# Router loads from ScalarE's queue, and two expert tiles ahead of the first rows, in a two-layer hybrid decoder

## The chip, the cores and the metric

The kernel runs on one core of a Trainium2 chip. The metric is device time in microseconds (us). All times inside a run come from one profiled execution, counted from the start of its span. The five engines are TensorE (PE, with its weight loads as PEld), VectorE (DVE), ScalarE (ACT), GpSimd (POOL) and SyncE (SP), which here issues DMA. Three queues carry most DMA: q1 is what SP issues, q10 what ScalarE issues, q0 what GpSimd issues; 16 DMA engines serve them all.

## What is computed

Two residual layers on 1024 tokens of width 1024, all in float32. The first mixes by attention, the second by a state-space layer and gated DeltaNet; both are followed by a mixture of experts and a gated embedding. What matters here:

```python
for i in range(DEPTH):                      # DEPTH = 2
    a = _rms_norm(h, norm_mix[i])
    ...
    h = h + mixer(a) @ w_out                # even_mixer or odd_mixer
    h = h + _hier_moe(_rms_norm(h, norm_ffn[i]), ...)
    h = h + _per_layer_embedding(h, p[i], ...)

def _hier_moe(m, ...):
    g_prob = softmax(m @ w_group + b_group)           # 4 groups, the best one is taken
    e_logits = (m @ w_expert + b_expert)[group]       # 8 experts in it, the best two are taken
    ...
    return _expert_dispatch(xf, experts, weights, w_gate, w_up, w_down)
    # each expert: (silu(x @ w_gate[e]) * (x @ w_up[e])) @ w_down[e]
```

There are 32 experts; the three weight matrices of one are 2 MB each.

## The kernel before

Tokens lie in 8 tiles of 128 rows (`NT`), a row's 1024 columns in two halves of 512 (`SLAB`). Engines meet only at semaphores; a block ends with a barrier of all engines. The order within an engine is the order of the code.

`mixer_end` is one block, run once a layer. For each tile i TensorE multiplies the mixer's output by `w_out`, half by half (`product(i, 0, ...)` with slab 0, `product(i, 1, ...)` with slab 1, eight steps k each), VectorE adds the residual (`add`), which SP loads into `h` in four pairs of tiles. TensorE transposes the sum (`turn`), ScalarE and VectorE copy the two halves (`copy`), and TensorE multiplies by the router weights `w` (`score`). VectorE multiplies `w` once by the gain column first (`scale_router`, in the turn of tile 0, waits for all five small loads, `router_in`). ScalarE squares the sum for the norm (`square`, `root`); VectorE scales a tile by norm and gains into `m` (`scale`), picks two experts for each token (`choose`) and numbers their slots (`place`), with ranks from TensorE (`rank_tokens`). GpSimd scatters the rows of the tile to `slots_in` in HBM. For the last tile ScalarE multiplies by the norm and GpSimd by the gains (L1542).

In the second layer (`delta`) half of the product's input must first be normed (`scale_o` on VectorE, with `root_o` on ScalarE), transposed on TensorE (`turn_o`) and copied on ScalarE (`copy_o`).

After the last tile come small steps on 32 experts: they are sorted by count, and `r.table` is written, whose row 3 holds which expert has which rank (L1511). SP waits for the scatters and reads the first two experts' rows (L1231). `keep_busy` issues products of the identity into a bank that nobody reads.

What SP issues in `mixer_end`, in this order: slab 1, `h`, gains and the five router loads (L1217 to L1222), then own loads (L1226): the first six weight tiles of the experts, four of them at once in the first layer and three in the second, the rest when the last products are done.

`first_blocks` computes the experts in 21 units. Weight tiles pass through a ring of eight places in the order of `weight_order`. The six tiles of experts 0 and 1 (`FIXED`) are the own loads; from number 6 on SP reads the expert's index from `r.table` and issues each tile when TensorE has finished with what lies in its place:

```python
before = [x for x in range(n) if places[x] == places[n]]
if before:
    used, by = tiles[before[-1]][0], last_user[tiles[before[-1]]]
    sp.wait_ge((gated, upped, downed)[used], (2 if used == 2 else 1) * (by + 1))
```

TensorE's first instruction there is the transpose of unit 0's rows (`turn(0)`, L1760), which waits for the read of L1231. In the trace a gate or up tile shows as `in_moe_w_gate_dram` or `in_moe_w_up_dram`, a down tile as `in_moe_w_down_dram`; tiles of the ring lie in `place`, `xt`, `s_t`, `own`, `gdn_t`, `work` and `gbz`.

Of the kernel before, what the change touches and what calls it, by code (L numbers as in the profile page):

```python
# [15 lines left out]
P = 128  # L16
# [139 lines left out]
def row(ap1d):  # L156

    return ap1d.rearrange("(a n) -> a n", a=1)
# [843 lines left out]
def even_mixer(nc, c, t, h, layer, r, xt, s5_t, after):  # L1002
# [5 lines left out]
    with ExitStack() as ctx:  # L1008
# [14 lines left out]
        def pair_out(heads):  # L1023
# [19 lines left out]
        mixer_end(nc, c, t, layer, h, t["x"][0], lambda k, i: mixed_t[k][:, i], slabs, [(slabs[1], slab_of(t["ev_w_out"][j], SLAB))], m, normed, mt, spare,  # L1043
                  preloads(t, layer, ring), 4, r, ch, gains=gains)
# [7 lines left out]
def constants(nc, ctx):  # L1052
# [10 lines left out]
    c.scattered_before = [0] * 4  # L1063
    c.rows_in = [ctx.enter_context(nc.semaphore(f"rows_in{n}")) for n in range(4)]
# [13 lines left out]
EARLY = 6  # L1078
# [77 lines left out]
def mixer_end(nc, c, t, layer, h, residual, columns, slabs, slab_loads, first_rows, m, mt, spare, own_loads, early_loads, r, ch, delta=None, gains=None):  # L1156
# [10 lines left out]
    with ExitStack() as ctx:  # L1167
        if gains is None:
# [29 lines left out]
        names = ("residual0_in", "residual1_in", "residual2_in", "residual3_in", "slabs_in", "router_in", "gain_in", "own_in", "iota_done",  # L1198
                 "o_means", "o_roots", "o_scaled", "o_turned", "o_copied", "products", "added", "squares", "means",
                 "roots", "rstd_made", "normed", "scaled", "router_scaled", "turns", "copied_act", "copied_dve", "scored", "taken_two", "ranked", "placed", "counted", "shifted",  # L1200
                 "exped", "sorted_at", "tabled", "positions", "positions_turned", "earlier_made", "spread_out", "vec_steps")
        with stage(nc, *names) as (block, sems):
# [6 lines left out]
            def _(sp):  # L1209
                with nc.allow_non_contiguous_dma(reason="router weights, short rows, column slabs"):  # L1210
                    for tile, view in slab_loads:
                        sp.dma_start(tile, view).then_inc(z["slabs_in"], 16)
                    sp.dma_start(h[:, 0:2], residual.rearrange("(t p) d -> p t d", p=P)[:, 0:2]).then_inc(residual_in[0], 16)
                    for n in range(1, 4):
                        two = slice(2 * n, 2 * n + 2)
                        sp.dma_start(h[:, two], residual.rearrange("(t p) d -> p t d", p=P)[:, two]).then_inc(residual_in[n], 16)
                    sp.dma_start(gains, row(t["norm_ffn"][layer]).to_broadcast([P, D])).then_inc(z["gain_in"], 16)  # L1217
                    sp.dma_start(gain_col[:], t["norm_ffn"][layer].rearrange("(k p) -> p k", p=P)).then_inc(z["router_in"], 16)
                    sp.dma_start(w[:, :, 0:GROUPS], t["moe_w_group"][layer].rearrange("(k p) n -> p k n", p=P)).then_inc(z["router_in"], 16)
                    sp.dma_start(w[:, :, GROUPS:ROUTES], t["moe_w_expert"][layer].rearrange("(k p) n -> p k n", p=P)).then_inc(z["router_in"], 16)  # L1220
                    sp.dma_start(bias[:, 0:GROUPS], row(t["moe_b_group"][layer]).to_broadcast([P, GROUPS])).then_inc(z["router_in"], 16)
                    sp.dma_start(bias[:, GROUPS:ROUTES], row(t["moe_b_expert"][layer]).to_broadcast([P, EXPERTS])).then_inc(z["router_in"], 16)  # L1222
# [12 lines left out]
            def _(pe):  # L1235
# [8 lines left out]
                def product(i, n, ks):  # L1244
                    if i and ks[0] == 0:
                        pe.wait_ge(z["added"], 2 * (i - 1) + n + 1)
                    if i == 0 and n == 1 and ks[0] == 0 and slab_loads:
                        pe.wait_ge(z["slabs_in"], 16 * len(slab_loads))
# [54 lines left out]
                keep_busy(pe, c, o_bank, 24)  # L1303
# [13 lines left out]
                keep_busy(pe, c, o_bank, 10)  # L1317

            @block.scalar
            def _(act):  # L1320
# [16 lines left out]
                def square(i, n):  # L1337
                    half = slice(n * SLAB, (n + 1) * SLAB)
                    act.wait_ge(z["added"], 2 * i + n + 1)
                    if n == 0 and i >= RING_M:  # L1340
                        act.wait_ge(scattered[i % RING_M], before[i % RING_M] + 32 * (i // RING_M))
                    act.activation(m[:, i % RING_M, half], h[:, i, half], ACT.Square, scale=1.0 / math.sqrt(D), accum_out=half_ms[:, i, n:n + 1]).then_inc(z["squares"], 1)
# [5 lines left out]
                if delta is not None:  # L1348
                    root_o(0)
                    copy_o(0)  # L1350
                for i in range(NT):
# [7 lines left out]
                    root(i)  # L1359
                act.wait_ge(z["rstd_made"], NT)  # L1360
                act.activation(m[:, (NT - 1) % RING_M, :], h[:, NT - 1, :], ACT.Copy, scale=rstd[:, NT - 1:NT]).then_inc(z["normed"], 1)
# [5 lines left out]
            def _(dve):  # L1367
# [26 lines left out]

                def scale(i):
                    if i == 0:
                        dve.wait_ge(z["gain_in"], 16)
# [65 lines left out]
                for i in range(NT):  # L1463
# [3 lines left out]
                    if i:  # L1467
                        choose(i - 1)
                        place(i - 1)
# [2070 lines left out]
```

## Time and profile before

| What | us |
|---|---|
| median of 3 runs | 2957.79 |
| lowest, highest | 2955.67, 2961.13 |
| the profiled execution | 2960.23 |
| its span | 2958.6 |
| TensorE busy | 2760.8 (93%) |
| TensorE weight loads busy | 1417.6 (48%) |
| VectorE busy | 1090.9 (37%) |
| ScalarE busy | 674.3 (23%) |
| GpSimd busy | 229.4 (8%) |

`mixer_end` starts at about 660 us in the first layer and 2100 us in the second; `first_blocks` starts at about 819 and 2263. The page shows each engine's busy time in 40 slices of the span, and what DMA moved: 404 to 418 GB/s in the slices that lie wholly in the experts' stages. A busy share is an average over stages; what a change is worth is read at the waits of its own stage. In a row of the timeline the bracket tells how long the engine was idle before it and what released it.

### The profile page before, as it was taken

Reading aid. Unit: us, or ns where it says so; the run is one execution under the profiler, and the core shown is the slowest. Engines: PE = TensorE matmul, PEld = TensorE weight load, DVE = VectorE, ACT = ScalarE, POOL = GpSimd, SP = SyncE. Lnnn points to the kernel's source line nnn. Section 1 sums busy time; section 2 is a strip of 40 time slices with the busy share of each in tenths; the row PEclk is TensorE's granted clock in tenths of the full one; section 3 lists DMA queues with packets and bytes.
Section 4 is the critical chain, followed back from the end, with each engine's and each line's share of the span. In section 5 each row is a group of like instructions: output and inputs, shape, how many; then the busy total and the mean of one; then the engine's idle time right before and its main releaser. Section 6 shows DMA issues by size and latency. Waiting matters only on the chain. (4 is left out here: it accounts for less than half of the span.)

```text
span 2958.6 us, 41299 instructions
## 1 busy us (share of the span) xinstructions
PE 2760.8 (93%) x16673; PEld 1417.6 (48%) x16674; DVE 1090.9 (37%) x2394; ACT 674.3 (23%) x1312; POOL 229.4 (8%) x288
## 2 busy tenths in 40 slices
PE   8999999999999999999989899988999989999998
PEld 5544555555543233334457744488655323232344
DVE  3585455553510000004456635555563000000053
ACT  3310354541110000002420123333211000000132
POOL 0000000000100000002000000055211000000020
PEclk9999999999999999999999999999999999999999
DMA  4000693006399999997110120000517999999931
GB/s 167 29 29 0 244 408 116 1 19 233 127 344 409 412 409 411 409 414 278 43 47 29 17 72 29 0 3 25 200 57 266 387 408 409 406 413 404 392 129 43
DMA packets 139127, 609.40 MB, mean 206 GB/s; under 512 B 27780, under 2 KB 34340, under 8 KB 122536
## 3 DMA queue, kind: packets, MB, share of 16 engines
q1 hardware_dynamic: 115976, 529.59, 45.7%
q0 software_dynamic: 15296, 53.49, 4.9%
q10 hardware_dynamic: 7664, 23.66, 2.1%
q8 instruction: 134, 2.20, 0.3%
q14 instruction: 57, 0.47, 0.0%
HBM read 503.81 MB, written 101.71 MB: 205 GB/s over the span
## 5 line engine op out<-in xcount | busy, mean ns | idle before, releaser
L2857 PE MATMUL acc<-xt,work 128*128 128x512 f32 x384 | 166.9, 593 | 0.0
L695 PE MATMUL acc<-h,xt 128*128 128x512 f32 x384 | 165.2, 592 | 0.0
L328 PE MATMUL scores<-xt 65*128 65x512 f32 (+7 forms) x384 | 146.0, 489 | 0.4 <-DVE xt L469 0.4
L1768 PE MATMUL pu<-place 128*32 128x512 f32 (+2 forms) x912 | 141.4, 628 | 0.6 <-issue 0.6
L1768 PE MATMUL py<-place 128*32 128x512 f32 (+2 forms) x672 | 126.5, 615 | 12.5 <-issue 12.4
L1768 PE MATMUL pg<-place 128*32 128x512 f32 (+1 forms) x528 | 130.4, 594 | 0.0
L475 DVE TENSOR_REDUCE nmax<-scores 128x1 f32<-128x256 f32 (+7 forms) x128 | 96.8, 757 | 73.9 <-PE scores L330 71.8
L1252 PE MATMUL acc<-place 128*128 128x512 f32 x256 | 118.0, 605 | 2.5 <-DMA place<-in_ev_w_out_dram 1.4
L695 PEld LDWEIGHTS acc<-h,xt 128*128 128x128 f32 x384 | 72.9, 190 | 91.1 <-issue 90.9
L2857 PEld LDWEIGHTS acc<-xt,work 128*128 128x128 f32 x384 | 72.0, 190 | 86.1 <-issue 86.1
L1863 DVE COPY work<-py 128x512 f32<-128x512 f32 x21 | 14.5, 692 | 226.6 <-PE py L1768 226.6
L1863 DVE COPY place<-py 128x512 f32<-128x512 f32 x21 | 14.5, 692 | 225.4 <-PE py L1768 225.4
L422 ACT ACTIVATE s_t<-scores,nmax 128x256 f32<-128x256 f32 (+7 forms) x128 | 94.3, 737 | 8.0 <-DVE nmax L475 6.6
L792 ACT ACTIVATE place<-acc 128x256 f32<-128x256 f32 (+4 forms) x88 | 39.9, 473 | 239.6 <-PE acc L695 239.5
L2505 PE MATMUL acc<-s_t,xt 128*128 128x260 f32 (+1 forms) x256 | 85.4, 495 | 1.1 <-PEq L71 1.1
L1896 DVE TENSOR_TENSOR work<-work,pu 128x512 f32<-128x512 f32 x21 | 14.4, 687 | 192.5 <-PE pu L1768 192.5
L1896 DVE TENSOR_TENSOR place<-place,pu 128x512 f32<-128x512 f32 x21 | 14.4, 688 | 189.4 <-PE pu L1768 189.4
L1768 PEld LDWEIGHTS py<-place 128*32 128x32 f32 (+2 forms) x672 | 39.8, 120 | 89.1 <-issue 87.8
L1842 ACT ACTIVATE work<-pg 128x512 f32<-128x512 f32 x21 | 12.5, 597 | 290.7 <-PE pg L1768 290.7
L328 PEld LDWEIGHTS scores<-xt 65*128 65x128 f32 (+1 forms) x384 | 62.8, 190 | 33.1 <-issue 32.7
L1842 ACT ACTIVATE place<-pg 128x512 f32<-128x512 f32 x21 | 12.5, 597 | 289.2 <-PE pg L1768 289.2
L1768 PE MATMUL pg<-own,work 128*32 128x512 f32 (+2 forms) x400 | 74.0, 599 | 3.6 <-issue 2.5
(755 smaller groups left out, 5467.1 us busy)
## 6 DMA issues: line engine op xcount, KB each, us to landing
place<-in_moe_w_up_dram SPq DMA_DIRECT2D x25, 2048.0 KB, 25.7
slots_out<-zeros SPq DMA_DIRECT2D x4, 9216.0 KB, 63.0
place<-in_moe_w_down_dram SPq DMA_DIRECT2D x18, 2048.0 KB, 25.8
xt<-in_moe_w_up_dram SPq DMA_DIRECT2D x17, 2048.0 KB, 25.3
xt<-in_moe_w_gate_dram SPq DMA_DIRECT2D x16, 2048.0 KB, 23.9
place<-in_moe_w_gate_dram SPq DMA_DIRECT2D x16, 2048.0 KB, 23.4
xt<-in_moe_w_down_dram SPq DMA_DIRECT2D x15, 2048.0 KB, 27.6
s_t<-in_moe_w_gate_dram SPq DMA_DIRECT2D x10, 2048.0 KB, 24.3
```

The source lines that it names most:

```text
L328: pe.matmul(bank(n, u)[:, a * SLAB:a * SLAB + w], qkt[0:kind(p).rows, p % 2, u, 0, i * P:(i + 1) * P], qkt[0:kind(p).rows, p % 2, u, 1, a ...
L422: act.activation(probs[:, u, n % 2, 0:(i + 1) * P], bank(n, u), ACT.Exp, bias=nmax[:, n % 2, u:u + 1], accum_out=total[:, (n // NT) % 2, i ...
L475: dve.tensor_reduce(nmax[:, n % 2, u:u + 1], bank(n, u), AX.X, ALU.max, negate=True).then_inc(maxed, 1)
L695: last = pe.matmul(acc[:, n % 4, 0:width], xs[:, k, tile_of(i)], weights[:, k, cols], start=(k == 0), stop=(k == k_of - 1))
L792: last = act.activation(place, part, ACT.Copy)
L1252: last = pe.matmul(acc[:, n, :], columns(k, i), slabs[n][:, k, :], start=(k == 0), stop=(k == KD - 1), skip_group_check=True)
L1768: last = pe.matmul(out[part], lhs[:, k, part], weights_of(kind, q)[:, k, cols], start=(k == 0), stop=(k == k_last), skip_group_check=True)
L1842: act.activation(gate, pg[:], ACT.Silu).then_inc(silued, 1)
L1863: dve.tensor_copy(y[:, n % 2, SLAB:D], py[:, SLAB:D]).then_inc(y_dve, 1)
L1896: dve.tensor_tensor(hid, gate, pu[:], ALU.mult).then_inc(hidden, 1)
L2505: ins = pe.matmul(acc[:, n % 4, 0:width], xt[:, k, at], slab[:, k, 0:width], start=(k == 0), stop=(k == KD - 1))
L2857: last = pe.matmul(acc[:, n % 4, :], slabs[m // 4 % 2][:, k, (m % 4) * P:(m % 4 + 1) * P], xt[:, k, half * SLAB:(half + 1) * SLAB], start= ...
```

## The change

Both layers, in `mixer_end` and at its seam with `first_blocks`:

- SP no longer issues gains and router loads; ScalarE does, ahead of its loop over the tiles (in the second layer behind `root_o(0)` and `copy_o(0)`). SP's own loads follow directly on `h`.
- Slab 1 comes in two DMAs of four steps k each, with a semaphore each.
- In the second layer `turn_o(0)` stands behind the first four products.
- `square` writes its unused output to a PSUM bank, `junk`, and no longer to `m`; the wait for the scatter moves to `scale`.
- For the last tile VectorE multiplies the sum by the gains in two halves (`gain_last`) before the norm is known, ScalarE then by the norm, and GpSimd's product goes.
- The table's row 3 is written first, with a semaphore `listed`. SP waits for it, reads two indices and issues ring tiles 6 and 7 (`LISTED`), then waits for the scatters and reads the first rows. `first_blocks` starts at tile 8.
- Three `keep_busy` runs: 24 becomes 16, 10 becomes 5; those of 5 and 8 stay.

```diff
             @block.sync
...
-                    for tile, view in slab_loads:
-                        sp.dma_start(tile, view).then_inc(z["slabs_in"], 16)
...
-                    sp.dma_start(gains, row(t["norm_ffn"][layer]).to_broadcast([P, D])).then_inc(z["gain_in"], 16)
-                    sp.dma_start(gain_col[:], t["norm_ffn"][layer].rearrange("(k p) -> p k", p=P)).then_inc(z["router_in"], 16)
...
+                    sp.dma_start(slabs[1][:, 0:4], last_slab[:, 0:4]).then_inc(z["slab_head_in"], 16)
+                    sp.dma_start(slabs[1][:, 4:8], last_slab[:, 4:8]).then_inc(z["slab_tail_in"], 16)
...
                 clear_used(sp)
+                views = expert_weights(t, layer)
+                sp.wait_ge(z["listed"], 1)
+                for n, (tile, kind, q) in enumerate(listed_loads):
+                    expert = sp.value_load(r.table[0:1, 3, q:q + 1], min_val=0, max_val=EXPERTS - 1)
+                    sp.dma_start(tile, views[kind][expert]).then_inc(c.listed_in[n], 16)
                 for n in range(RING_M):
                     sp.wait_ge(scattered[n], c.scattered_before[n])
...
-                if delta is not None:
-                    turn_o(0)
                 for i in range(NT):
                     product(i, 0, range(0, 4))
                     if i:
                         turn(i - 1, 1)
+                    elif delta is not None:
+                        turn_o(0)
...
-                    act.activation(m[:, i % RING_M, half], h[:, i, half], ACT.Square, scale=1.0 / math.sqrt(D), accum_out=half_ms[:, i, n:n + 1]).then_inc(z["squares"], 1)
+                    act.activation(junk[:], h[:, i, half], ACT.Square, scale=1.0 / math.sqrt(D), accum_out=half_ms[:, i, n:n + 1]).then_inc(z["squares"], 1)
...
                 if delta is not None:
                     root_o(0)
                     copy_o(0)
+                with nc.allow_non_contiguous_dma(reason="router weights, short rows"):
+                    act.dma_start(gains, row(t["norm_ffn"][layer]).to_broadcast([P, D])).then_inc(z["gain_in"], 16)
+                    act.dma_start(gain_col[:], t["norm_ffn"][layer].rearrange("(k p) -> p k", p=P)).then_inc(z["router_in"], 16)
+                    act.dma_start(w[:, :, 0:GROUPS], t["moe_w_group"][layer].rearrange("(k p) n -> p k n", p=P)).then_inc(z["router_in"], 16)
+                    act.dma_start(w[:, :, GROUPS:ROUTES], t["moe_w_expert"][layer].rearrange("(k p) n -> p k n", p=P)).then_inc(z["router_in"], 16)
...
+                def gain_last(n):
+                    i, half = NT - 1, slice(n * SLAB, (n + 1) * SLAB)
...
+                    dve.tensor_tensor(m[:, i % RING_M, half], h[:, i, half], gains[:, half], ALU.mult).then_inc(z["gained"], 1)
...
                 dve.wait_ge(z["tabled"], 1)
+                dve.tensor_copy(r.table[:, 3, E], acc[0:1, 1, EXPERTS:2 * EXPERTS]).then_inc(z["listed"], 1)
                 step(dve.tensor_copy(over, acc[0:1, 1, E]))
-                step(dve.tensor_copy(r.table[:, 3, E], acc[0:1, 1, EXPERTS:2 * EXPERTS]))
...
-                        pool.tensor_tensor(m[:, i % RING_M, :], m[:, i % RING_M, :], gains[:], ALU.mult).then_inc(z["scaled"], 1)
```

SP's queue at the start of `mixer_end` in the first layer, before:

```order
L1212 DMA place<-in_ev_w_out_dram 128x8x512
L1213 DMA h<-in_x_dram 128x2x1024
L1216 DMA h<-in_x_dram 128x2x1024 x3
L1217 DMA place<-in_norm_ffn_dram 128x1024
L1218 DMA gain_col<-in_norm_ffn_dram 128x8x1
L1219 DMA w<-in_moe_w_group_dram 128x8x4
L1220 DMA w<-in_moe_w_expert_dram 128x8x32
L1221 DMA bias<-in_moe_b_group_dram 128x4
L1222 DMA bias<-in_moe_b_expert_dram 128x32
L1226 DMA xt<-in_moe_w_gate_dram 128x4096
L1226 DMA xt<-in_moe_w_up_dram 128x4096
```

and after, down to the own loads that wait for the last products:

```order
L1213 DMA place<-in_ev_w_out_dram 128x4x512
L1214 DMA place<-in_ev_w_out_dram 128x4x512
L1217 DMA h<-in_x_dram 128x2x1024 x4
L1221 DMA xt<-in_moe_w_gate_dram 128x4096
L1221 DMA xt<-in_moe_w_up_dram 128x4096
L1221 DMA place<-in_moe_w_down_dram 128x4x1024
L1221 DMA s_t<-in_moe_w_gate_dram 128x4096
L1221 DMA place<-in_moe_w_up_dram 128x4096 [waits products_194]
```

The six small loads have left SP; the four own tiles stand directly behind `h`. ScalarE at the start of `mixer_end` in the second layer, where `o_rms` is the root of `scale_o` and `xt<-o_bank` is `copy_o`, before:

```order
L1323 ACT_TABLE_LOAD
L1323 ACTIVATE o_rms<-o_ms 128x4
L1329 ACTIVATE xt<-o_bank 128x512
L1323 ACTIVATE o_rms<-o_ms 128x4
L1342 ACTIVATE work,half_ms<-h 128x512
```

and after:

```order
L1325 ACT_TABLE_LOAD
L1325 ACTIVATE o_rms<-o_ms 128x4
L1331 ACTIVATE xt<-o_bank 128x512
L1354 DMA gains<-in_norm_ffn_dram 128x1024
L1355 DMA gain_col<-in_norm_ffn_dram 128x8x1
L1356 DMA w<-in_moe_w_group_dram 128x8x4
L1357 DMA w<-in_moe_w_expert_dram 128x8x32
L1358 DMA bias<-in_moe_b_group_dram 128x4
L1359 DMA bias<-in_moe_b_expert_dram 128x32
L1325 ACTIVATE o_rms<-o_ms 128x4
L1344 ACTIVATE junk,half_ms<-h 128x512
```

Six DMA issues stand now between the first `xt` copy and the second `o_rms` root. SP's queue at the end of `mixer_end` in the first layer, before, across the barrier into `first_blocks`:

```order
L1226 DMA place<-in_moe_w_down_dram 128x4x1024 [waits products_192]
L64 ISA x23
L1231 DMA place<-slots_in 128x1024 [waits scattered2,scattered1,scattered0]
L1231 DMA place<-slots_in 128x1024
L74 UNCONDITIONAL_BRANCH [waits own_in_185]
L1711 UNCONDITIONAL_BRANCH [waits barrier_Pool_Activation_PE_DVE_SP_release]
L1717 TENSOR_LOAD table
L1717 ISA x2
L1722 ISA
L1722 DMA place<-in_moe_w_gate_dram 128x4096
```

and after, behind the same own load:

```order
L1226 TENSOR_LOAD table [waits listed_216]
L1226 ISA x2
L1227 ISA
L1227 DMA place<-in_moe_w_gate_dram 128x4096
L1226 TENSOR_LOAD table
L1226 ISA x2
L1227 ISA
L1227 DMA place<-in_moe_w_gate_dram 128x4096
L1231 DMA place<-slots_in 128x1024 [waits scattered2,scattered1,scattered0]
L1231 DMA place<-slots_in 128x1024
L74 UNCONDITIONAL_BRANCH [waits own_in_187]
```

The two gate tiles have moved from behind the barrier to ahead of the two reads of `slots_in`.

## Rows read from the trace of the kernel before

**Rows 1.** Timeline, first layer: start us, us, engine line op [idle before <-releaser].
```profile
684.33 0.46 DVE L1403 TENSOR_TENSOR w<-w,gain_col 128x288 f32<-128x288 f32 x1 [2.31 <-DMA bias<-in_moe_b_expert_dram]
...
684.85 2.02 PE L1271 MATMUL scores<-w,place 128*128 128x36 f32 x16 [1.02 <-DVE w L1403]
```

**Rows 2.** DMA of 857:859, 850:856, 869:871.5, 677.5:682.5 us: packets, MB, engine share.
```profile
q1 hardware_dynamic: 30, 0.49, 65.7%
q10 hardware_dynamic: 31, 0.13, 17.7%
...
q1 hardware_dynamic: 165, 2.42, 95.5%
...
q1 hardware_dynamic: 240, 0.98, 97.6%
...
DMA packets 3458, 0.87 MB, mean 174 GB/s; under 512 B 3293, under 2 KB 3293, under 8 KB 3455
...
q1 hardware_dynamic: 3458, 0.87, 82.6%
```

**Rows 3.** SP's timeline from 660 us, and the first pair's median us to landing.
```profile
660.88 0.58 SPq L1213 DMA_DIRECT2D h<-in_x_dram  x1
...
663.87 1.50 SPq L1217 DMA_DIRECT2D place<-in_norm_ffn_dram  x1
...
667.07 9.65 SPq L1219 DMA_DIRECT2D w<-in_moe_w_group_dram  x1
...
h<-in_x_dram SPq DMA_DIRECT2D x1, 1024.0 KB, 10.6
```

**Rows 4.** Timeline of ScalarE and TensorE at the second layer's start.
```profile
2107.57 0.21 ACT L1323 ACTIVATE o_rms<-o_ms 128x4 f32<-128x4 f32 x1 [2.51 <-DVE o_ms L1375]
...
2115.70 0.60 PE L1261 MATMUL turned<-ident,h 128*128 128x128 f32 x4
...
2127.31 1.87 PE L1271 MATMUL scores<-w,xt 128*128 128x36 f32 x16
```

**Rows 5.** Timeline from the first choice to the experts, first layer.
```profile
687.39 0.22 DVE L1413 SCALAR_TENSOR_TENSOR group_eq<-spare,gmax,rev 128x4 f32<-128x4 f32 x1
...
801.45 2.39 DVE L1413 SCALAR_TENSOR_TENSOR group_eq<-spare,gmax,rev 128x4 f32<-128x4 f32 x1
801.47 2.35 POOL L1542 TENSOR_TENSOR place<-place 128x1024 f32<-128x1024 f32 x1 [2.35 <-ACT place L1361]
...
812.21 0.18 DVE L1511 CAST table<-acc 1x32 int32<-1x32 f32 x1
...
819.61 1.14 PE L1760 MATMUL turned<-ident,place 128*128 128x128 f32 x8 [0.30 <-PEq L71]
...
820.53 1.47 SPq L1722 DMA_DIRECT2D place<-in_moe_w_gate_dram  x2
...
828.83 1.05 PE L1760 MATMUL turned<-ident,place 128*128 128x128 f32 x8
```

**Rows 6.** Second layer's seam; landings (last column); stretches with PEclk behind POOL's (x).
```profile
s_t<-in_moe_w_up_dram SPq DMA_DIRECT2D x1, 2048.0 KB, 9.1
xt<-in_moe_w_down_dram SPq DMA_DIRECT2D x1, 2048.0 KB, 16.9
...
2264.01 1.97 PE L1760 MATMUL turned<-ident,work 128*128 128x128 f32 x8 [1.31 <-DMA work<-slots_in]
...
2275.70 1.04 PE L1760 MATMUL turned<-ident,work 128*128 128x128 f32 x8
...
820.00:822.50 2.50, 1.39 (x9) 0.96 (x8) 2.29 (x7) 1.70 (x2) 0.17 (x1) 1.00 0.51 97
...
2265.00:2267.50 2.50, 1.39 (x6) 0.99 (x5) 2.26 (x8) 1.47 (x2) 0.21 (x1) 0.50 0.78 249
```

**Rows 7.** Landings: a tile alone (issued 2231), and the tile issued at 866.4.
```profile
work<-in_moe_w_gate_dram SPq DMA_DIRECT2D x1, 2048.0 KB, 8.2
...
place<-in_moe_w_down_dram SPq DMA_DIRECT2D x1, 2048.0 KB, 8.9
```

More of the change, by code:

```diff
@@ L1042, in even_mixer @@
         ring = own + [flat_fk, s5_t.rearrange("p k n -> p (k n)"), flat_fv] + behind
[L1043 to L1044 removed]
+        mixer_end(nc, c, t, layer, h, t["x"][0], lambda k, i: mixed_t[k][:, i], slabs, slab_of(t["ev_w_out"][j], SLAB), m, normed, mt, spare,
+                  preloads(t, layer, ring), 4, listed(ring), r, ch, gains=gains)
         moe(nc, c, t, layer, h, r, ch, ring, EARLY, m, (0, 1, 3), after)
@@ L1063, in constants @@
     c.scattered_before = [0] * 4
+    c.listed_in = [ctx.enter_context(nc.semaphore(f"listed_in{n}")) for n in range(LISTED)]
     c.rows_in = [ctx.enter_context(nc.semaphore(f"rows_in{n}")) for n in range(4)]
@@ L1077 @@
 RING = 8
-EARLY = 6
+EARLY, LISTED = 6, 2
 QUAD = P // 4
@@ L1209, in _ @@
             def _(sp):
-                with nc.allow_non_contiguous_dma(reason="router weights, short rows, column slabs"):
-                    for tile, view in slab_loads:
-                        sp.dma_start(tile, view).then_inc(z["slabs_in"], 16)
[L1213 to L1216, printed above, removed]
-                    sp.dma_start(gains, row(t["norm_ffn"][layer]).to_broadcast([P, D])).then_inc(z["gain_in"], 16)
-                    sp.dma_start(gain_col[:], t["norm_ffn"][layer].rearrange("(k p) -> p k", p=P)).then_inc(z["router_in"], 16)
[L1219 to L1222, printed above, removed]
+                with nc.allow_non_contiguous_dma(reason="column slabs"):
+                    sp.dma_start(slabs[1][:, 0:4], last_slab[:, 0:4]).then_inc(z["slab_head_in"], 16)
+                    sp.dma_start(slabs[1][:, 4:8], last_slab[:, 4:8]).then_inc(z["slab_tail_in"], 16)
+                for n in range(4):
+                    two = slice(2 * n, 2 * n + 2)
+                    sp.dma_start(h[:, two], residual.rearrange("(t p) d -> p t d", p=P)[:, two]).then_inc(residual_in[n], 16)
                 for n, (tile, view) in enumerate(own_loads):
@@ L1466, in _ @@
                     add(i, 0)
+                    if i == NT - 1:
+                        gain_last(0)
                     if i:
@@ L1470, in _ @@
                     add(i, 1)
+                    if i == NT - 1:
+                        gain_last(1)
                     if i < NT - 1:
@@ L1479, in _ @@
                 place(NT - 1)
-                dve.wait_ge(z["scaled"], NT)
+                dve.wait_ge(z["gained"], 2)
                 def wide(x, n):
@@ L1713, in _ @@
                 expert = {}
-                for n in range(preloaded, len(tiles)):
+                for n in range(preloaded + LISTED, len(tiles)):
                     kind, q = tiles[n]
@@ L1931, in preloads, with listed @@
             for n, (kind, q) in enumerate(tiles[0:EARLY])]
+def listed(ring):
+    _, units = expert_units()
+    tiles, places, _ = weight_order(units)
+    return [(ring[places[n]].rearrange("p (k n) -> p k n", k=FF // P if tiles[n][0] == 2 else KD), *tiles[n]) for n in range(EARLY, EARLY + LISTED)]
 class After:
```

42 lines of the change are left out of this document (27 added, 15 removed).

## The prediction

> **What bounds the kernel now.** One core, two layers, one chain. I read the page's slices first, then the issues and packets of the DMA queues, then the timeline at the two ends of `mixer_end` in each layer. TensorE is 93% busy, so only its idle stretches can be won or lost, and each layer has three. At the start of `mixer_end` it waits for router weights: in the first layer the first scores start at 684.85, 1.02 us late, on the scaled `w` [rows 1]. At its end comes a chain of small VectorE steps, the scatter of the last rows and the read of the first ones. Then the experts (`first_blocks`, 540 us a layer), where weights stream with the 16 DMA engines full and SP mostly waits for TensorE to free a ring tile.
>
> Two things about DMA decide this case. One queue serves in order: two tiles that SP issues back to back in the second layer land 9.1 and 16.9 us after issue [rows 6]. And queues that have work at the same time take turns packet by packet, whatever a packet's size: from 857 to 859 us SP's queue (q1) moved 30 packets in 0.49 MB (16 KB each), ScalarE's (q10) 31 in 0.13 MB (4 KB each) [rows 2]. The engines were full, so a 4 KB packet waited for a 16 KB one each time.
>
> **Part 1: the router loads go from SP's queue to ScalarE's.** Their number is the point. `gain_col`, `w` of the groups and `w` of the experts are 128 x 8 runs each (1,024 packets), the two biases and `gains` 128 each: 3,456 packets. Before, they pass through q1 in one go: 3,293 packets under 512 B sit in the 5 us from 677.5 to 682.5, where the engines were 82.6% busy (4.1 us); 165 larger ones of 4 KB take 0.68 MB / 0.40 = 1.7 of that (0.98 MB in 2.5 us at 97.6%), so all small ones cost 2.4 us [rows 2].
> After, they compete with what SP issues now without a pause: the slab (1,024 runs of 2 KB), `h` (1,024 of 4 KB) and four own tiles. A gate or up tile is about 128 packets (165 packets in 2.42 MB), a down tile 512 (240 in 0.98 MB, 4 KB each) [rows 2], so 128 x 3 + 512 = 896. q1 holds 2,944 packets, q10 3,456. With turns one for one q10 cannot finish before q1 has finished all four tiles. The router weights, wanted at 684, would land with the last of them.
> When: the first `h` pair is issued at 660.88 and lands 10.6 us later, 671.5 [rows 3]; behind it lie 3.15 MB of `h` and 8.39 MB of tiles, 28.9 us, then 1.3 us for `gains` and 2.4 for the small ones: 704.1. Small packets partly use gaps, so I take 702.5. VectorE's `scale_router` adds 0.5 (684.33 to 684.85) [rows 1]: scores at 703.0 instead of 684.85, **+18.1 us**. TensorE's clock dips after the wait in either kernel.
> Second layer: the same pair issued at 2100.5 lands at 2111.1 by the same row; three own tiles (6.29 MB) and 3.15 MB follow, 23.6 us, plus 3.7: 2138.4, taken as 2137. Scores at 2137.5 instead of 2127.3: **+10.2** at least.
> There the six issues also stand in front of work: ScalarE is free at 2105.06, and the next thing it does is the root at 2107.57 which VectorE's `scale_o(1)` needs, and behind that stands `add(0, 0)` and TensorE's `turn(0, 0)` (2115.70) [rows 4]. On SP the issue of `gains` took 1.50 us and that of the group weights 9.65 [rows 3], because a queue holds only so many packets: when that one got through, at 676.7, q1 had taken 4,224 and served about 2,000 (the slab, the `h` pair landed at 671.5 and 5.2 us more). If q10 holds some 2,200 too, ScalarE is held until 1,250 have been served, in turns with what is left of `h` and two tiles: until about 2129. Then the root (0.21) and three VectorE steps, about 2 us by my estimate: `turn(0, 0)` at 2130.9, +15.2, and up to 2.5 for a clock that has fallen (below): 17.7. If q10 holds all of it, 10.2 stands. I take the middle, **+14.0**; in the first layer ScalarE has nothing to do for some 11 us after the start, since its first work needs that `h` pair.
>
> **Part 2: the small steps.** `turn_o(0)` behind four products lets TensorE begin earlier in the second layer, and the split slab shortens a wait in the first, where the next instruction waits for `h` all the same. Both lie ahead of the later router wait, so they count nothing. `gain_last` fits where VectorE waits for TensorE. It takes GpSimd's product away, beside which VectorE's `group_eq` step took 2.39 us instead of 0.22 [rows 5]: 2.2 us off the chain to the table and to the scatter, in both layers. The next thing late is then SP.
>
> **Part 3: two tiles ahead of the first rows.** SP waits for the table (written 812.21, in the new order 0.2 earlier, less 2.2: 810.0), loads an index and issues; from the block's start to such an issue it needs 0.9 us (819.61 to 820.53) [rows 5], so 810.9. Then it waits for the scatters and issues the reads of the first rows, in the same queue behind 4.19 MB. One tile alone lands after 8.2 us [rows 7], the second 2.10 / 0.40 = 5.2 later, the first rows 1.3 after that: 825.6 instead of before 819.61: **+6.0**, with the 2.2 us gained already in. TensorE then has stood for 8 us and more. In the second layer it started this block at a granted 0.50 (1.2 GHz) and needed 11.69 us from first to second turn (2264.01 to 2275.70), in the first, at 1.00 (2.4 GHz) after junk products up to the wait, 9.22 (819.61 to 828.83) [rows 5, 6]. Junk products are fewer now, so the first layer pays **2.5 us** more. Second layer: q1 is busy with own tile 5 until 2241.2 + 16.9 = 2258.1 [rows 6]; two tiles and the rows behind it, 10.5 + 1.3: 2269.9 instead of 2264.0, **+5.9**.
> What do 10.5 us of transfer in an idle gap give back? Little. Ring tiles 8 onwards wait for TensorE's first units, which start late. The tile issued at 866.4 took 8.9 us, one alone 8.2 [rows 7]: nothing but 0.7 us was queued before it, so the stream hangs there on TensorE's time, and all behind it comes as late as TensorE. I count 0 and keep 0.7 a layer for the range.
>
> **Sum.** 18.1 + 14.0 + 6.0 + 2.5 + 5.9 = 46.5 us on the profiled execution's 2960.2: 3006.7. Its time is 2.4 over the median of 2957.8; on the median, **3004 us**.
>
> **Rivals.**
> (a) *Small packets don't take single turns.* If many runs of 4 to 128 B ride in one turn, the router weights land by about 675. `h` is late by at most 3.7 us in the first layer, the wait of 1.0 goes, ScalarE's hold of some 7 to 8 us puts `turn(0, 0)` of the second at about its old time: +2 for both starts. The end costs 14.4: 2974. Only packets of 4 KB and more are seen in turns in [rows 2]; against the rival speaks that size made no difference there. The Trainium skill, in "DMA: Bandwidth & Descriptors", section "SWDGE vs HWDGE vs iDMA", names as the boundary at which an engine changes queue a packet of preferably up to 4096 bytes and at most 64 descriptors, for the descriptors that GpSimd makes; by that rule 64 small runs an engine would be one turn, and the time this rival's. No run here shows it for small runs. Chance 0.22, by that rule.
> (b) *The row reads are not held up by the tiles.* Part 1 as forecast, the end gains 2.2 a layer: 32.1 - 4.4, so 2985. The landings one after another in q1 speak against it. 0.09.
> (c) *Faster.* The stream of weights, not TensorE, paces all of `first_blocks`: each layer ends earlier by the 10.5 us that two tiles take. It decides if the queue never runs empty after the first tiles, that is if the tile of 866.4 had had some 10 us queued before it; its 8.9 says no. With small packets prompt as in (a), 21 + 4.4 and the 1.0 us of the first scores: 2931. 0.06.
> (d) Either half of part 1 alone, or a hold twice as long: 2990, or 3020 and over. 0.08.
> Forecast 0.55, spread by the second layer's start (10.2 to 17.7), by 701 to 704 for the first, and by 2 us of contention with the scatters: 2994 to 3014.
>
> **How the numbers follow.** What a measurement can tell from no change is 0.2%, 6 us. Slower: 0.55 + 0.22 + 0.09 + 0.08 = 0.94, less 0.03 for an (a) whose end costs little: 0.91; faster 0.06; same 0.03. The range takes in forecast, (b) and most of (a): 2966 to 3018.
>
> **What would show it.** Right: q10 still at work on small packets when the fourth own tile lands (near 702), TensorE idle before the first scores for 15 us and more in the first layer and some 10 in the second; DMA issues on ScalarE of 5 us and more in the second layer with VectorE's reciprocal waiting; `group_eq` at 0.22; the first rows' reads 9 us and more from issue to landing; after that the experts' stage as long as before. Wrong: router weights landed by 680 (a), row reads landing within 4 us (b), or an experts' stage shorter by 5 us or more (c).

## The result and the profile after

The changed kernel took 3020.05 us (median of 4, 3018.33 to 3022.95), the kernel before beside it 2959.46 (2955.67 to 2962.87): ratio 1.0206, 95% interval 1.0188 to 1.0224. The forecast was 3004 with a range up to 3018. The direction was right, and the causes named for the loss are in the traces. One step was wrong: how long ScalarE is held by its own queue in the second layer. The time came out 16 us above the forecast, the loss of 60.6 us 14 us above the forecast 46.5.

Some words for what follows. The start of a layer's `mixer_end` is judged by the last turn of token tile 2, when the waits for router weights are over. The seam is the stretch from the last turn of token tile 7 to the experts' second turn (`turn(1)`). ScalarE is held while one of its DMA issues has not gone through, so that the work behind it waits. Two queues take turns when each gets one packet through in alternation.

The profiled spans are 2958.6 and 3016.7 us, 58.1 apart. Cut at places that exist in both traces, the 58.1 are:

| stretch | before | after | difference | forecast |
|---|---|---|---|---|
| up to the last turn of token tile 2, first layer | 716.46 | 736.97 | +20.5 | +18.1 |
| last turn of token tile 7 to the experts' second turn, first layer | 30.56 | 39.99 | +9.4 | +6.0 + 2.5 |
| from there to the end of the first experts' stage | 523.94 | 524.55 | +0.6 | 0 |
| code that is the same, up to SP's first issue in the second `mixer_end` | 747.29 | 749.07 | +1.8 | 0 |
| from there to the last turn of token tile 2, second layer | 58.04 | 79.24 | +21.2 | +14.0 |
| last turn of token tile 7 to the experts' second turn, second layer | 34.04 | 41.70 | +7.7 | +5.9 |
| second experts' stage, and what is left | | | -3.1 | 0 |

The first layer's start, in the timeline of ScalarE's queue and of TensorE (start us, us, then the idle time before it and what ended it); the row answers to [rows 1], where the same wait was 1.02:

```profile
661.88 8.95 ACTq L1357 DMA_DIRECT2D w<-in_moe_w_expert_dram  x1
670.86 15.87 ACTq L1358 DMA_DIRECT2D bias<-in_moe_b_group_dram  x1
686.76 2.96 ACTq L1359 DMA_DIRECT2D bias<-in_moe_b_expert_dram  x1
689.76 0.60 ACT L1344 ACTIVATE junk<-h 128x512 f32<-128x512 f32 x1 [30.61 <-issue]
...
704.09 3.63 PE L1273 MATMUL scores<-w,place 128*128 128x36 f32 x16 [15.89 <-DVE w L1422]
```

TensorE stands for 15.9 us, ScalarE spends 29.5 in its six issues (660.18 to 689.72). What the 16 DMA engines do meanwhile (packets, MB, share), from 671 to 681 us with `h` in q1 and from 681 to 690 with own tiles:

```profile
q1 hardware_dynamic: 974, 3.92, 100.4%
q10 hardware_dynamic: 974, 0.01, 6.0%
...
q1 hardware_dynamic: 255, 3.84, 100.7%
q10 hardware_dynamic: 255, 0.00, 1.6%
```

974 against 974, 255 against 255: one packet of 4 to 16 bytes for one of 4 KB, and then for one of 15 KB on the average. It is what [rows 2] showed for 4 and 16 KB, now at up to a thousandfold ratio of sizes.

The second layer's start. The same six issues stand in front of the root that VectorE waits for, and TensorE behind both ([rows 4] has the root at 2107.57 with 2.51 idle, the turn at 2115.70 with none):

```profile
2136.57 0.34 ACTq L1354 DMA_DIRECT2D gains<-in_norm_ffn_dram  x1
...
2141.63 16.10 ACTq L1357 DMA_DIRECT2D w<-in_moe_w_expert_dram  x1
2157.75 7.33 ACTq L1358 DMA_DIRECT2D bias<-in_moe_b_group_dram  x1
...
2165.61 0.20 ACT L1325 ACTIVATE o_rms<-o_ms 128x4 f32<-128x4 f32 x1 [28.45 <-issue]
...
2167.47 1.11 PE L1263 MATMUL turned<-ident,h 128*128 128x128 f32 x4 [23.12 <-DVE h L1396]
...
2180.92 1.87 PE L1273 MATMUL scores<-w,xt 128*128 128x36 f32 x16
```

`turn(0, 0)` comes 35.1 us after SP's first issue in this block (2132.38), 15.6 before: 19.5 of the 21.2 us are ScalarE's hold. The other 1.8 come behind it: the granted clock is 0.64 from 2167.5 to 2172.5. The first scores wait for nothing here. The last router load lands at 2169.4, after the hold but 11 us before them. Nor does ScalarE stand behind SP's issues: SP's last one here ends at 2140.8.

The seams. The rows are TensorE's first turns of both experts' stages, the landing of the last scatters and of the rows in the second (last column), and a stretch after the first (PEclk behind POOL's count), to hold against [rows 5, 6]:

```profile
846.97 1.97 PE L1783 MATMUL turned<-ident,place 128*128 128x128 f32 x8 [12.17 <-DMA place<-slots_in]
...
858.76 1.05 PE L1783 MATMUL turned<-ident,place 128*128 128x128 f32 x8
...
2325.26 1.97 PE L1783 MATMUL turned<-ident,work 128*128 128x128 f32 x8 [13.46 <-DMA work<-slots_in]
...
work<-slots_in SPq DMA_DIRECT2D x2, 512.0 KB, 9.4
slots_in<-work,slots POOLq DMA_INDIRECT x4, 10.8
...
847.00:849.50 2.50, 1.94 (x8) 1.54 (x8) 0.00 (x0) 0.52 (x1) 0.00 (x0) 0.50 0.02 7
```

The reads of the first rows take 13.9 us in the first layer and 9.4 in the second from issue to landing behind two tiles, 3.8 and 3.7 before. In the first layer it is 11.8 us from first to second turn, 9.2 before: the granted clock at the first turn is 0.50, the lower level of 1.2 GHz, and was 1.00.

### The profile page after: what moved, and what is told of

It reads as the page before. It is cut to its first block and busy times, and to the rows that moved or that the text cites. A ratio compares the mean times of both kernels' runs of the same rounds, so it can differ in the third digit from the quotient of the medians.

```text
span 3016.7 us, 41253 instructions
## 1 busy us (share of the span) xinstructions
PE 2757.1 (91%) x16621; PEld 1411.0 (47%) x16622; DVE 1088.6 (36%) x2398; ACT 673.8 (22%) x1312; POOL 223.6 (7%) x286
## 5 line engine op out<-in xcount | busy, mean ns | idle before, releaser
L328 PEld LDWEIGHTS scores<-xt 65*128 65x128 f32 (+1 forms) x384 | 62.8, 190 | 33.1 <-issue 32.7
L1865 ACT ACTIVATE place<-pg 128x512 f32<-128x512 f32 x21 | 12.5, 597 | 292.4 <-PE pg L1791 292.4
L1791 PE MATMUL pg<-xt,place 128*32 128x512 f32 (+2 forms) x400 | 74.1, 599 | 3.5 <-issue 2.4
## 6 DMA issues: line engine op xcount, KB each, us to landing
xt<-in_moe_w_gate_dram SPq DMA_DIRECT2D x16, 2048.0 KB, 22.7
```

What stands on the lines that cost most here:

```text
L328: pe.matmul(bank(n, u)[:, a * SLAB:a * SLAB + w], qkt[0:kind(p).rows, p % 2, u, 0, i * P:(i + 1) * P], qkt[0:kind(p).rows, p % 2, u, 1, a ...
L1791: last = pe.matmul(out[part], lhs[:, k, part], weights_of(kind, q)[:, k, cols], start=(k == 0), stop=(k == k_last), skip_group_check=True)
```

## Experiments

All ratios are to the kernel before, run beside them; about 2959 us. Edits are against the changed kernel where nothing else is said, and shortened: `...` stands for lines left out, and ends of long lines are missing.

**1. The changed kernel without part 1.**

```diff
-                    act.dma_start(gains, ...)   # and the five router loads
+                    sp.dma_start(gains, ...)    # behind the reads of h, as before
```

> The changed kernel with part 1 undone: the six loads of gains, router weights and biases stand on SP's queue again, behind the reads of h and ahead of the own tiles. Turns theory (q1 and q10 take turns packet for packet, and ScalarE is held by its full queue): both starts come back to the times of before, so that only the two seams stay, which in the trace of the changed kernel cost 6.9 + 2.6 us in the first layer (first turn, and clock up to the second turn) and 7.7 in the second: 17 us over the kernel before, about 2976, ratio 1.006 (1.004 to 1.008). Rival (the seams are dear only because the starts left the weight stream late, or the starts are late because of the split slab or the moved turn_o): then most of the 60 us would stay, ratio 1.01 and over. Rival (tiles pay back in the experts' stage once the start is clean): 1.001 or less.

Measured: 2981.59, ratio 1.0074 (1.0059 to 1.0090), inside the expected range, though 5.7 us above the 17 expected, and clear of both rivals. In the trace the last turn of token tile 2 is at 718.18 in the first layer and 61.5 us after SP's first issue in the second (before 716.46 and 58.0): the starts are nearly back, the seams are 40.60 and 41.96. Part 1 thus costs 38 of the 60 us. The starts do not come back to zero; experiments 3 and 9 are on that.

**2. The changed kernel without part 3.**

```diff
-EARLY, LISTED = 6, 2
+EARLY, LISTED = 6, 0
...
-                sp.wait_ge(z["listed"], 1)
-                for n, (tile, kind, q) in enumerate(listed_loads):
...
```

> The changed kernel with part 3 undone: no listed tiles ahead of the first rows (their count is 0, the experts' stage loads them itself). Turns theory: both starts stay late, 20.5 us in the first layer and 21.2 in the second as in the changed kernel's trace, and the two seams turn from a loss of 17 to a gain of 2.2 each (GpSimd's product is gone): 41.7 - 4.4 = 37 us over before, about 2996, ratio 1.0126 (1.011 to 1.014). Rival (the router wait of part 1 ends in the same slack as the seam's, so that the parts do not add up): ratio below 1.009 or the whole 1.02.

Measured: 2998.66, 1.0136 (1.0121 to 1.0152), inside the expected range. The parts add up: 22.7 us without part 1 and 39.8 without part 3, less the 1.3 of part 2 (experiment 3, not to be told from zero) that both hold, is 61; the whole change is 60.6.

**3. Part 2 alone.**

```diff
-                    act.dma_start(gains, ...)   # and the five router loads
+                    sp.dma_start(gains, ...)
...
-EARLY, LISTED = 6, 2
+EARLY, LISTED = 6, 0
```

> Parts 1 and 3 undone; left are the split slab, the moved turn_o, the square into a psum tile, gain_last on VectorE in place of GpSimd's product, the table written first and fewer junk products. Forecast of the prediction: group_eq of the last token tile at 0.22 us, the spread 2.2 us earlier after the last product in each layer, the first rows too: 4.4 us faster, ratio 0.9985 (0.9975 to 0.9995). Rival (fewer junk products let TensorE's clock drop before the experts' first products): up to 2.5 a layer back, ratio 1.000 (0.9995 to 1.001).

Measured: 2960.11, 1.0002 (0.9993 to 1.0011), the rival's value. Its gain is in the trace and is lost again. In the first layer:

```profile
815.72 1.94 PE L1778 MATMUL turned<-ident,place 128*128 128x128 f32 x8 [0.69 <-PEq L71]
...
828.18 1.05 PE L1778 MATMUL turned<-ident,place 128*128 128x128 f32 x8
...
815.70:818.20 2.50, 1.94 (x8) 1.56 (x8) 2.31 (x6) 0.50 (x1) 0.00 (x0) 0.50 0.72 166
```

The first turn comes 3.9 us earlier than in [rows 5], the second 0.65 earlier: the stretch between them starts at a granted 0.50 and takes 12.5 us, not 9.2. In the second layer the first turn waits 4.40 for the rows (1.31 before), and from first to second turn it is 12.9 for 11.7. At that layer's start the scores waited 2.75 us and the product behind them took 6.04.

**4. The same queue, but own tiles only after the router weights.**

```diff
+                sp.wait_ge(z["router_in"], 80)
+                sp.wait_ge(z["gain_in"], 16)
                 for n, (tile, view) in enumerate(own_loads):
```

> The changed kernel with one wait more: SP issues the own tiles only when gains and router weights have landed. The same six loads still go through ScalarE's queue, beside the slab and h alone (2,048 packets in q1 in the first layer, 1,024 in the second, in place of 2,944 and 1,792). Turns theory: q10's 3,456 packets need the partner packets only while there are such; router weights land near 683 in the first layer (704 in the changed kernel) and ScalarE is let go near 678; in the second it is let go some 10 us after its first issue instead of 28.6. Starts cost 0 to 4 us each instead of 20.5 and 21.2, the seams stay: 18 to 25 us over before, ratio 1.007 (1.006 to 1.0085). Rival (the issue of 3,456 small packets itself holds ScalarE for 28 us, whatever else the engines do, as writing the descriptors is slow there): the second start stays at +20, the first loses 5 to 10: ratio 1.013 and over.

Measured: 2987.07, 1.0102 (1.0087 to 1.0118), between the expected value and the rival's. The first start is healed (scores at 685.59 with no wait, 704.09 in the changed kernel). ScalarE was still held in the second, 16.7 us in place of 29.0, and TensorE waited 10.86:

```profile
2118.47 8.83 ACTq L1359 DMA_DIRECT2D w<-in_moe_w_expert_dram  x1
...
2130.99 0.21 ACT L1327 ACTIVATE o_rms<-o_ms 128x4 f32<-128x4 f32 x1 [16.18 <-issue]
```

The issue of the same packets is thus not what takes 28 us; it gets shorter with less in q1. My count had left out the slab there: q1 still held 2,048 packets, not 1,024. The second start is 9.2 us longer than before, in place of 21.2.

**5. The same bytes in a third of the packets, on ScalarE's queue.**

```diff
-act.dma_start(gain_col[:], t["norm_ffn"][layer].rearrange("(k p) -> p k", p=P))
...
-act.dma_start(w[:, :, GROUPS:ROUTES], t["moe_w_expert"][layer].rearrange("(k p) n -> p k n", p=P))
+act.dma_start(gain_col[:].rearrange("p (h k) -> p h k", h=2), t["norm_ffn"][layer].rearrange("(h p k) -> p h k", h=2, p=P))
+act.dma_start(w_expert.rearrange("p (h k) -> p h k", h=2), t["moe_w_expert"][layer].rearrange("(h p k) n -> p h (k n)", h=2, p=P))
...
-pe.transpose(..., h[:, i, k * P:(k + 1) * P], c.ident[:])
+pe.transpose(..., h[:, i, n * SLAB:(n + 1) * SLAB].rearrange("t (p k) -> t k p", k=4)[:, k % 4], c.ident[:])
```

> The changed kernel with the same router weights in fewer packets. Row r of the weights goes to partition (r mod 512) div 4 in place of r mod 128, so that four rows are one run (64 and 512 B), and the turns of h take every fourth column to match: gain_col and the two weights are 256 packets each in place of 1,024, with the biases and gains 1,152 in place of 3,456, the same bytes on ScalarE's queue beside the same slab, h and own tiles. VectorE scales in two steps instead of one. Turns theory: q10 is through after 1,152 turns, near 671 in the first layer, and never full: ScalarE is free after 3 us, both starts cost 0 to 2 us instead of 20.5 and 21.2, and the first scores wait for nothing, so that some 4 to 6 us less than the kernel with parts 2 and 3 come out (there the scores of the second layer still waited 3.46 us and the clock fell): 12 to 20 us over before, ratio 1.0055 (1.004 to 1.007). Rival (what delays is that a second queue shares the 16 engines at all, or the bytes): both starts stay late, ratio 1.014 and over.

Measured: 2989.37, 1.0103 (1.0089 to 1.0118): slower than expected, and short of the rival's 1.014. The first start costs 1.4 us in place of 20.5, the second 6.7 in place of 21.2. ScalarE's six issues take 3.0 us in place of 29.0 in the second layer, and `turn(0, 0)` waits 1.13 in place of 23.12. But the scores behind it wait 5.59, since q10 began 4 us behind q1 and its last packets met the own tiles (2139 to 2144 us):

```profile
q1 hardware_dynamic: 144, 2.10, 98.4%
q10 hardware_dynamic: 141, 0.02, 2.2%
```

One packet each again. The hold and the late weights can now be told apart, and with the same bytes in the same queue both shrink with the count of packets.

**6. The packed loads on SP's queue, with part 2.**

```diff
# against experiment 5
-act.dma_start(w_expert..., 4 rows to a run)   # and the five others
+sp.dma_start(w_expert..., 4 rows to a run)    # behind the reads of h
...
-EARLY, LISTED = 6, 2
+EARLY, LISTED = 6, 0
```

> Part 2 alone (parts 1 and 3 undone) with the packed router loads, on SP's queue. In the run of part 2 alone the scores of the second layer waited 2.75 us for the router weights, the clock fell and the next product took 6.04 instead of 3.7 us; in the first layer they waited 1.02. With 1,152 packets SP's issue of the group weights (9.96 us there) is short and the weights land right behind h: these waits and the fallen clock go, 1 to 2 us in the first layer and 5 to 7 in the second: 6 to 8 us less than part 2 alone, ratio 0.998 to before (0.9965 to 0.999). Rival (the waits are only moved to the gains or the fourth h pair): ratio 1.000.

Measured: 2951.68, **0.9973** (0.9964 to 0.9982), as expected, and faster than both kernels. No scores wait: the last turn of token tile 2 comes at 713.68, and 54.6 us after SP's first issue in the second layer (58.0 before). The seams are 29.1 and 33.1 (30.6 and 34.0 before). Together these four are 8.6 us shorter, which is what the medians show. The way from the last turn of token tile 2 to that of token tile 7 is 0.3 us longer in both layers (82.1 for 81.8, 83.9 for 83.6); the turns of every fourth column may be why, which no run tests.

**7. Both on ScalarE's queue**: packed loads, and own tiles behind them.

```diff
 # experiment 5, and
+                sp.wait_ge(z["router_in"], 80)
+                sp.wait_ge(z["gain_in"], 16)
```

> The changed kernel with both cures: the packed router loads (1,152 packets) on ScalarE's queue, and SP's own tiles behind their landing. In packed_on_act alone the first scores of the second layer still waited 5.59 us, since the last 400 packets of q10 took turns with 16 KB packets of the own tiles (141 against 144 from 2139 to 2144 us); in own_behind alone ScalarE was still held for 16.7 us in the second layer. Theory: each cure takes away what the other left, both starts are as with the packed loads on SP (54.6 us in the second layer, first layer's turn of token tile 2 at 714 to 716), and only the seams of part 3 stay, 10.8 + 8.1 us over the 0.9973 of packed_on_sp: 10 to 14 us over before, ratio 1.004 (1.003 to 1.005). Rival (ScalarE's queue costs something of its own in either start, whatever it shares): 1.007 and over.

Measured: 2976.31, 1.0056 (1.0039 to 1.0073). The interval takes in the expected 1.004 and the rival's 1.007, so the time does not decide; the trace speaks for a little of the rival. The second start is 55.9, 1.3 longer than with the packed loads on SP. In the first it costs 4.0 (717.63 for 713.68): `turn(0, 0)` comes 2.3 later (`gains` now goes beside the first `h` pair, which I take for the reason; no run shows it), and from there to the next turn it is 9.2 us for 7.5. The rest is part 3: seams of 40.8 and 42.2 for 29.1 and 33.1.

**8. The two tiles behind the reads of the first rows**, router loads on SP.

```diff
# against experiment 1
+                for n in range(RING_M):
+                    sp.wait_ge(scattered[n], c.scattered_before[n])
+                for n in range(2):
+                    sp.dma_start(first_rows[:, n, :], ...)
                 sp.wait_ge(z["listed"], 1)
                 for n, (tile, kind, q) in enumerate(listed_loads):
...
-                for n in range(RING_M):
-                    sp.wait_ge(scattered[n], c.scattered_before[n])
-                for n in range(2):
-                    sp.dma_start(first_rows[:, n, :], ...)
```

> Part 1 undone, and the two listed tiles issued behind the reads of the first rows, still before the experts' stage begins. If part 3 costs what it does because the rows queue behind 4.19 MB in q1, its 10.8 and 8.1 us (turn 15 to the second turn of the experts) are gone and the time is that of part 2 alone, 1.0002 (0.999 to 1.0012), as the tiles come some 3 us earlier than in the experts' stage and nothing waits for them. Rival (an idle gap filled with tiles shortens the experts' stage): 0.9985 and less. Rival (the scatters and the wait for them are what the listed tiles delay, wherever they stand): 1.004 and over.

Measured: 2957.42, 0.9995 (0.9987 to 1.0004), as expected. The seams are 29.78 and 34.08, for 40.60 and 41.96 in experiment 1, which differs in this order alone: what part 3 costs is the place in the queue. Whether the tiles bring anything there can't be told from zero; the experts' stages take 524.6 and 522.1 us, in the other kernels 521.8 to 525.5.

**9. `turn_o` moved, and nothing else.**

```diff
# against the kernel before
-                if delta is not None:
-                    turn_o(0)
...
                     if i:
                         turn(i - 1, 1)
+                    elif delta is not None:
+                        turn_o(0)
```

> The kernel before with one move from part 2: turn_o(0) behind the first four products of token tile 0. In the run of part 2 alone the second layer's start, from SP's first issue to the turn of token tile 2, took 60.6 us for 58.0 before: TensorE began its products 3.2 us earlier, then waited 2.75 us for the router weights at the first scores, which came only 0.8 us earlier, and at half clock the next product took 6.04 us. Theory: the move alone does that, since the weights land when they did, and is 2.6 us slower in the second layer and nothing in the first: ratio 1.0009 (1.000 to 1.0018). Rival (something else of part 2 costs this, the move gives what it was meant to give): ratio 0.999.

Measured: 2960.37, 0.9999 (0.9990 to 1.0008), between the expected value and the rival's, so the time confirms neither. The trace shows the mechanism: TensorE is early, waits 3.22 us for the weights, and the scores and the product behind them run longer than in the kernel before (3.38 us for 1.87, 5.64 for 3.7).

```profile
2126.69 3.38 PE L1271 MATMUL scores<-w,xt 128*128 128x36 f32 x16 [3.22 <-DVE w L1403]
2129.87 5.64 PE L1252 MATMUL acc<-work,s_t 128*128 128x512 f32 x8
```

That start took 61.0 us (58.0 before), and 61.5, 60.6, 58.9 and 58.3 in the traces of experiments 1, 3, 10 and 8, which hold the same move. The loss varies with the wait and with what follows it: in experiment 8 the scores waited 2.02 us and took 1.98. With the packed loads of experiment 6 the same move waits for nothing and the start takes 54.6 us.

**10. Part 2 with the junk products of before** (24 and 10).

```diff
# against experiment 3
-                keep_busy(pe, c, o_bank, 16)
+                keep_busy(pe, c, o_bank, 24)
...
-                keep_busy(pe, c, o_bank, 5)
+                keep_busy(pe, c, o_bank, 10)
```

> Part 2 alone with the junk products of before (24 and 10 in place of 16 and 5). In part 2 alone the first layer's spread came 2.14 us earlier (811.97 for 814.11), the first turn 3.9 (815.72), but the experts' second turn only 0.65 (828.18 for 828.83): the clock stood at half, 12.46 us between the two for 9.22 before. With the junk back the clock is up at the first turn, which comes later by 1.5 to 2 us as the last junk products end later: 1 to 2 us less than part 2 alone, ratio 0.9997 (0.999 to 1.0005). Rival (the clock there falls because TensorE idles before the spread, whatever junk follows): no change against part 2 alone.

Measured: 2959.08, 1.0002 (0.9991 to 1.0012): the same as part 2 alone, though an interval that takes in the expected 0.9997 too. The first layer's first turn came at 818.42, 2.7 us later, and the second at 829.27, with 1.6 us less between them. The granted clock behind the first turn was 0.94, not 0.50. The rival's value is thus right and its reason is not: the junk does keep the clock up, and the longer junk run makes the first turn later by more than the clock gives back.

**11 and 12. The packed loads on SP with the tiles behind the rows, and then own tile 5 behind them too.**

```diff
 # 11: experiments 6 and 8 together, LISTED = 2
 # 12: the same, and
-EARLY, LISTED = 6, 2
+EARLY, LISTED = 5, 3
```

> Packed router loads on SP (0.9973 with part 2) and the two listed tiles behind the reads of the first rows (0.9995 with part 2, 1.0002 without). If both are independent: 0.9967 (0.996 to 0.998). Rival (the tiles behind the rows bring nothing): 0.9973 as before.

> The same as packed_rows_first, but own tile 5 (the down weights of expert 1, 2.10 MB) no longer ahead of the scatters and first rows but behind the reads of the first rows, with the two listed tiles (5 own tiles, 3 behind). In the second layer it was issued with the last product, landed 16.9 us later, and the last scatters (8.5 us, 5.2 in the first layer) and the first rows stood beside and behind it, so that the 2.2 us gained on VectorE in part 2 were lost there. Theory: the second seam (turn 15 to the experts' second turn, 33.1 to 34.0 us) shrinks by 3 to 5 us, the first layer stays within 1: ratio 0.9953 (0.9945 to 0.9965). Rival (the scatters' own time, not the queue, sets the first rows, or the tile then comes too late for its first use and TensorE waits there): 0.9965 and over.

Measured: 2954.53, 0.9982 (0.9973 to 0.9991), and 2953.29, 0.9979 (0.9970 to 0.9988). Both miss the expected values (0.9967 and 0.9953) and go with the rivals, the first just at the end of its interval: tiles behind the rows bring nothing that these runs can show, and the later tile 5 nothing more. Neither beats experiment 6, and their intervals overlap with its. In experiment 12 the second seam did shrink, from 33.4 to 30.5 us (3 to 5 less expected); the second experts' stage took 1.7 more and the first seam 0.6.

## Why the prediction was right or wrong

**What held.** *Turns, packet for packet*: shown at 4 to 16 bytes against 16 KB, and by experiment 5 it is the count that matters. Rival (a), the turn of many small packets, is out; the last of the router loads landed at 703.6 (issued 686.76, 16.8 us to landing), forecast 702.5. The rule of the Trainium skill it leaned on ("DMA: Bandwidth & Descriptors", section "SWDGE vs HWDGE vs iDMA": up to 64 descriptors to a turn, for those that GpSimd makes) is not what these two queues show (974 against 974). *Part 3* delays the rows by their place in q1 (experiment 8); rival (b) is out. *No give-back* was right: the experts' stages changed by +0.6 and -1.2; rival (c) is out.

**The step that failed** is how long ScalarE's full queue holds it in the second layer, the term "I take the middle, +14.0": the start measured 21.2, over the term's own upper bound of 17.7. Two things were wrong in it.

The middle was wrong because the case at the lower bound, q10 taking all 3,456 packets at once, does not occur. That is 3.7 of the 7.2 us that this term was short.

And the upper bound was too low. It let ScalarE go 24 us after it was free, when 1,250 packets of a queue of 2,200 are served; it was 28.4 (2137.2 to 2165.6). The issue of the expert weights did end near that rule, at 2157.7 with 1,170 packets served (in the first layer at 670.8 with 980). What it had not reckoned with is the next issue, `b_group`, of only 128 packets: 7.3 us more here, until 1,620 were served, and 15.9 us in the first layer, until 2,140 were. A total of free places does not describe the queue; what does is open. The hold is 4.4 us of the miss; the fallen clock added 1.8, within the forecast 2.5.

**Smaller misses.** First start, 20.5 for 18.1: the scores begin 1.1 us later than forecast, and they and the product behind them run longer (3.63 us for 2.02 the scores alone), at the lower clock. "TensorE's clock dips after the wait in either kernel" hid that it dips longer after 15.9 us than after 1.0: a granted 0.50 from 686.8 to 690 before, 0.50 from 704 to 708 and 0.72 to 712 after. ScalarE's hold cost nothing there, as said, but not because it was short: it lasted to 689.8, and still ended 14 us before the scores. First seam: first turn +6.9 for +6.0, clock +2.6 for +2.5. Second seam, 7.7 for 5.9: the last scatters took 10.8 us beside the tiles, 8.5 before, so that the rows' read was issued late; this contention stood in the range, not in the sum. The other stretches, whose code is the same or which were put at 0, add up to -0.7.

**Part 2** "counts nothing" held in the whole change. As for `gain_last`, 2.2 us off the chain is right (`group_eq` 0.22, spread 2.3 earlier after the last turn in both layers), but alone it did not shorten the kernel. In the first layer the lower clock behind it took it back; in the second the first turn came only 1.4 us earlier after a longer wait for the rows, and the way to the second turn took 1.2 more. The other moves of part 2 were put at nothing because they lie ahead of the router wait; without part 1 the moved `turn_o` made that wait and the slow stretch behind it longer (experiment 9).

The range missed by 2 us. The forecast's own spread ended at 3014 and the range at 3018; "3020 and over" had been named under (d), and left out. The spread is also wider than the terms it names, which add up to some 7 us either way, not 10. And the rates given for the experts' stages ahead of the prediction are misread: the page's slices show 404 to 414 GB/s and one 387. The sums take 0.40 MB per us from [rows 2] and do not rest on them.

## What to carry to other kernels

Before you move small loads to a queue of their own, count packets, not bytes: beside a stream of big tiles each small packet waits for a big one, and once there are too many for the queue (3,456 here, not 1,152) the engine that issues them stands meanwhile. Make runs longer first (four rows of a weight to a partition, with the matching stride in the transposes), which paid in either queue here. What the next stage reads first goes ahead of everything that is only early, even into an idle gap. And where a cost lies between two bounds, ask whether the cheap end can happen at all before you take the middle.

## What the runs showed that was not expected

- A load of 2 KB (`b_group`, 128 packets) took 31.3 us from issue to landing in the changed kernel's first layer; with 1,152 packets for the queue its issue took 0.66 us, with 3,456 it took 15.87, and with 3,456 but no own tiles in q1 8.25.
- A gain of some 3 us ahead of a stretch in which TensorE idles can come to nothing, if the stretch then starts at 1.2 GHz (815.72 to 828.18 in place of 819.61 to 828.83).
- Unchanged code between the first experts' stage and the second `mixer_end` took 747.3 us in the trace before and 748.8 to 755.7 in the others. A sum made on one trace has that much noise in it, so a few us of difference between two spans should be looked for in the stretch that changed.
